# Rearranging u tile by tile, and moving the S5 steps two slots up, in a three-block fp32 kernel

## What is computed

```python
def s5_ssd_layer(h, w_in, ...):
    p = h @ w_in
    z = p[..., :o1]
    y_a = s5_mixer(p[..., o1:o2], ...)           # u: 1024 channels, 64 groups of 16
    y_a = y_a * silu(z[..., :S5_WIDTH])
    y_b = ssd_mixer(p[..., o2:o3], p[..., o3:], ...)
    y_b = rmsnorm_3(y_b * silu(z[..., S5_WIDTH:]), ssd_norm_w, SSD_GROUPS)
    return concatenate([y_a, y_b], -1) @ w_out

def s5_mixer(u, ...):
    # per group of 16 channels a complex diagonal recurrence with 64 states
    x_t = a * x_{t-1} + (coef * B) @ u_t
    y_t = real(C @ x_t)
    y = gelu(y + d_skip * u)
    return y * sigmoid(y @ glu_w + glu_b)
```

## Time and profile before

| | |
|---|---|
| median of 3 runs | 2980.46 us (2978.59 to 2983.39) |
| the profiled execution | 2977.42 us |
| its span | 2974.8 us |
| mean granted TensorE clock | 0.968 of full speed |
| TensorE matmul busy | 2803.0 us, 94% |
| VectorE, ScalarE, GpSimd busy | 48%, 34%, 38% |
| DMA | 286.21 MB, 96 GB/s; 34384 of 114251 packets under 512 B |
| `ab_in` (slots 0 to 35) | 2031.4 to 2309.3 us of the span |

### The profile page before, as it was taken

The page is one execution under the profiler, slowest core; times in us unless marked ns, Lnnn a source line. Parts: engine busy times, 40 slices in busy tenths (PEclk is TensorE's granted clock), DMA queues, the critical chain, the costliest instruction groups (busy, mean ns, idle before and its releaser), DMA issues. The chain is left out here.

```text
span 2974.8 us, 38973 instructions
## 1 busy us (share of the span) xinstructions
PE 2803.0 (94%) x16650; PEld 2300.7 (77%) x16650; DVE 1426.6 (48%) x1768; ACT 999.7 (34%) x1373; POOL 1129.7 (38%) x487
## 2 busy tenths in 40 slices
PE   7899999895899999999899999998799899999997
PEld 6778876794688888777788888886688668888785
DVE  5874338535448443873633442215287645333332
ACT  4233233113333332346432433222333644222441
POOL 3334443500244444364344444444233423322342
PEclk9999999996899999999999999999899999999998
DMA  5444222000133332222232233334855312222232
GB/s 195 148 129 148 97 94 78 31 4 1 62 113 131 110 109 90 87 91 85 71 100 92 92 99 94 98 99 144 135 163 150 105 61 89 82 65 66 69 99 71
DMA packets 114251, 286.21 MB, mean 96 GB/s; under 512 B 34384, under 2 KB 45584, under 8 KB 113424
## 3 DMA queue, kind: packets, MB, share of 16 engines
q1 hardware_dynamic: 114080, 283.74, 31.1%
HBM read 261.91 MB, written 24.15 MB: 96 GB/s over the span
## 5 line engine op out<-in xcount | busy, mean ns | idle before, releaser
L426 POOL TENSOR_TENSOR weight_ring_r<-weight_ring,weight_hi_r 128x1024 fp32r<-128x1024 f32 (+2 forms) x412 | 1043.0, 2532 | 1684.0 <-ACT weight_hi_r L419 1684.0
L419 ACT ACTIVATE weight_hi_r<-weight_ring 128x1024 fp32r<-128x1024 f32 (+2 forms) x412 | 447.7, 1088 | 1492.6 <-PE acc L629 1120.4
L623 PE MATMUL acc<-p_r,weight_hi_r 128*128 128x512 f32 x1776 | 701.4, 395 | 28.9 <-ACT weight_hi_r L419 19.4
L624 PE MATMUL acc<-scr_r,weight_hi_r 128*128 128x512 f32 x1120 | 440.5, 393 | 0.0
L629 PE MATMUL acc<-p_r,weight_ring_r 128*128 128x512 f32 x1776 | 436.6, 389 | 0.0
L623 PEld LDWEIGHTS acc<-p_r,weight_hi_r 128*128 128x128 f32 x1776 | 336.8, 190 | 103.5 <-ACT weight_hi_r L419 20.7
L624 PE MATMUL acc<-p_r,weight_hi_r 128*128 128x512 f32 x1008 | 392.1, 389 | 0.0
L629 PEld LDWEIGHTS acc<-p_r,weight_ring_r 128*128 128x128 f32 x1776 | 333.7, 188 | 69.5
L624 PEld LDWEIGHTS acc<-scr_r,weight_hi_r 128*128 128x128 f32 x1120 | 213.1, 190 | 46.1 <-issue 2.6
L623 PE MATMUL acc<-scr_r,weight_hi_r 128*128 128x512 f32 x544 | 220.2, 405 | 2.2 <-ACT weight_hi_r L419 2.2
L878 DVE SCALAR_TENSOR_TENSOR x<-acc,x 128x512 f32<-128x512 f32 x56 | 36.8, 687 | 381.9 <-PE acc L629 381.9
(11 more groups left out here) (542 smaller groups left out, 3872.7 us busy)
## 6 DMA issues: line engine op xcount, KB each, us to landing
weight_ring<-in_weights SPq DMA_DIRECT2D x372, 512.0 KB, 3.5
weight_ring<-in_weights SPq DMA_DIRECT2D x32, 704.0 KB, 4.0
weight_ring<-in_weights SPq DMA_DIRECT2D x8, 640.0 KB, 3.9
s_inner<-p SPq DMA_DIRECT2D x16, 256.0 KB, 4.3
s_outer<-p SPq DMA_DIRECT2D x16, 256.0 KB, 4.6
s_inputs<-p SPq DMA_DIRECT2D x16, 256.0 KB, 2.6
p<-s_inputs SPq DMA_DIRECT2D x8, 512.0 KB, 5.6
p<-s_inner SPq DMA_DIRECT2D x8, 512.0 KB, 4.9
```

The source lines that it names most:

```text
L419: self.nc.scalar.activation(self.r.weight_hi[:, ahead, 0:width], self.weight_ring[:, r, 0:width], ACT.Copy)\
L426: self.nc.gpsimd.tensor_tensor(rest, raw, hi, ALU.subtract).then_inc(self.weights_split, 1)
L623: pe.matmul(product.out(b, m), hi, op.hi(kx), start=kx == 0, stop=False)
L624: pe.matmul(product.out(b, m), hi, op.lo(kx), start=False, stop=False)
```

## The change

u is written to DRAM by place: for each of the eight tiles, as soon as its pair is evicted, eight DMAs (one for each place) put 128 rows of 64 numbers into `u_by_place` (SP slots 5 to 12), and in SP slots 7, 9, 11 and 13 one DMA each reads a quarter back, 4 KB from each row. The plain copy to `lift` moves to SP slots 14 to 17. V, K, the scan and Y move up: V by six to two slots, K and the scan by two, Y from twice in slots 27 and 28 to once in each of 25 to 28. `dve_skip` works in place without strides, and `act_gelu` reads with the stride and writes in token order. The dt transposes move from behind (9, 3) to behind (10, 1), the last row from (10, 1) to (10, 3). Chunk 0 of the SSD uses the odd buffers and comes first: its sums are read in SP slot 37, masked on GpSimd behind the rest of slot 35, and its exps run in the first slot of the GLU product.

```diff
@@ tables of places @@
-V_AT = ((12, 3), (13, 1), (13, 3), (14, 1))
-K_AT = ((14, 3), (15, 1), (15, 3), (16, 1), (16, 3), (17, 1), (17, 3), (18, 1))
-Y_AT = ((27, 1), (27, 3), (28, 1), (28, 3))
-SCAN_AT = {15: 2, 16: 2, 17: 2, 18: 1, 19: 2, 20: 1, 21: 2, 22: 1, 23: 2, 24: 1, 25: 1}
+V_AT = ((6, 3), (8, 3), (11, 3), (12, 1))
+K_AT = ((12, 3), (13, 1), (13, 3), (14, 1), (14, 3), (15, 1), (15, 3), (16, 1))
+Y_AT = ((25, 1), (26, 1), (27, 1), (28, 1))
+SCAN_AT = {13: 2, 14: 2, 15: 2, 16: 1, 17: 2, 18: 1, 19: 2, 20: 1, 21: 2, 22: 1, 23: 1}
@@ S5Layer.sp_slot @@
-        if at in (6, 8, 10, 12):
-            b = (at - 6) // 2
-            sp.wait_ge(core.freed["dve"], self.product.freed[b])
+        if 5 <= at < 13:
+            self.place_u(sp, at - 5)
+        if at in (7, 9, 11, 13):
+            b = (at - 7) // 2
+            sp.wait_ge(self.rows_out[b], 16 * 2 * S5_L)
+            u = core.dram["u_by_place"].rearrange("l i g n -> (l i) g n")
+            sp.dma_start(self.ul[:, 2 * S5_NB * b:2 * S5_NB * (b + 1), :], u[:, 2 * S5_NB * b:2 * S5_NB * (b + 1), :]).then_inc(self.rows_in[b], 16)
+        if 14 <= at < 18:
+            b = at - 14
             sp.dma_start(core.dram["lift"][2 * b * P:(2 * b + 2) * P, :].rearrange("(c p) t -> p c t", p=P),
                          core.p[:, S5_LIFT + 2 * b:S5_LIFT + 2 * b + 2, :]).then_inc(core.lifted, 16)
-        if at == 13:
-            sp.wait_ge(core.lifted, 16 * 4)
-            by_place = core.dram["lift"].rearrange("(g i) (l n) -> l i g n", i=S5_IN, l=S5_L)
-            for l in range(S5_L):
-                sp.dma_start(self.ul[l * S5_IN:(l + 1) * S5_IN], by_place[l]).then_inc(q["ul"], 16)
@@ S5Layer, new @@
+    def place_u(self, sp, c):
+        sp.wait_ge(self.core.freed["dve"], self.product.freed[c // 2])
+        by_place = self.core.dram["u_by_place"].rearrange("l i g n -> l g i n")
+        for l in range(S5_L):
+            sp.dma_start(by_place[l, S5_NB * c:S5_NB * (c + 1)], self.core.p[:, S5_LIFT + c, l * S5_N:(l + 1) * S5_N]).then_inc(self.rows_out[c // 2], 16)
@@ S5Layer.dve_skip, act_gelu @@
-        v.scalar_tensor_tensor(out=core.p[:, S5_GELU + c, :].rearrange("p (n l) -> p n l", l=S5_L), in0=by_run(self.u_again(c)),
-                               scalar=core.vcol("s5_d", c), in1=by_run(core.p[:, S5_UL + c, :]), op0=ALU.mult, op1=ALU.add).then_inc(self.q["skipped"], 1)
+        y = core.p[:, S5_UL + c, :]
+        v.scalar_tensor_tensor(out=y, in0=self.u_again(c), scalar=core.vcol("s5_d", c), in1=y, op0=ALU.mult, op1=ALU.add).then_inc(self.q["skipped"], 1)
-        self.core.nc.scalar.activation(y, y, ACT.Gelu_apprx_tanh).then_inc(self.q["gelu"], 1)
+        self.core.nc.scalar.activation(natural, lifted, ACT.Gelu_apprx_tanh).then_inc(self.q["gelu"], 1)
@@ SsdTimes.pe_part @@
-        if (at, part) == (9, 3):
+        if (at, part) == (10, 1):
             pe.wait_ge(q["sums"], 1)
+            pe.wait_ge(self.v_read, 4)
...
-        if (at, part) == (10, 1):
+        if (at, part) == (10, 3):
...
         if (at, part) == V_AT[0]:
+            pe.wait_ge(q["step"], 1)
+        if (at, part) == V_AT[2]:
             pe.wait_ge(q["exps"], 1)
@@ Ssd.sp_sums, GpSimd and ScalarE in block3_second @@
-            sp.wait_ge(layer.q["skipped"], DC)
+            sp.wait_ge(layer.q["gelu"], 2)
-    sums_at = {38: 1, 39: 0, 44: 2, 46: 3}
+    sums_at = {37: 0, 39: 1, 44: 2, 46: 3}
-                    if product is glu and at in (0, 1, 6):
-                        ssd.pool_mask(pool, {0: 1, 1: 0, 6: 2}[at])
+                    if (product, at) == (ab.product, 34):
+                        ssd.pool_mask(pool, 0)
+                    if product is glu and at in (1, 6):
+                        ssd.pool_mask(pool, {1: 1, 6: 2}[at])
+                if at == 0:
+                    ssd.act_exps(act, 0)
                 if at == 2:
-                    ssd.act_exps(act, 0)
+                    ssd.act_exps(act, 1)
                     ssd.act_copy(act, 0)
-                if at == 4:
-                    ssd.act_exps(act, 1)
```

More of the change, by code:

```diff
@@ L2706, in __init__ @@
         p, h, cst = core.p, core.h, core.cst
-        names = ("tables", "ul", "v", "v_read", "k", "k_read", "step", "y", "added", "u_back", "skipped", "gelu")
+        names = ("tables", "v", "v_read", "k", "k_read", "step", "y", "added", "u_back", "skipped", "gelu")
         self.q = {n: core.sem(f"sl_{n}") for n in names}
-        self.loaded, self.inner, self.outer = ([core.sem(f"sl_{n}{j}") for j in range(S5_PIECES)] for n in ("inputs", "inner", "outer"))
-        self.kept, self.back = ([core.sem(f"sl_{n}{j}") for j in range(S5_PIECES // 2)] for n in ("kept", "back"))
+        self.piece_in = [core.sem(f"sl_piece{j}") for j in range(S5_PIECES)]
+        self.rows_out, self.rows_in = ([core.sem(f"sl_rows_{n}{j}") for j in range(S5_PIECES // 2)] for n in ("out", "in"))
         flat = lambda a: a.rearrange("p a t -> p (a t)")
@@ L2740, in sp_slot @@
[L2740 to L2748 removed]
+        if at in (12, 13, 15, 16):
+            first = (0, 2, 4, 6)[(12, 13, 15, 16).index(at)]
+            for j in (first, first + 1):
+                sp.wait_ge(q["v"], j + 1)
+                sp.dma_start(self.place[j], piece("inner", j)).then_inc(self.piece_in[j], 16)
@@ L3459, in dve_slot @@
         layer = self.layer
-        if at in (27, 28, 29):
-            layer.dve_add(dve, (0, 2, 3)[at - 27])
+        if 25 <= at < 29:
+            layer.dve_add(dve, at - 25)
         if at == 35:
@@ L3589, in _ @@
             for s in core.flow_loads(sp, flow):
-                if s < ab.product.end:
+                if s < ab.product.end + RING:
                     ab.sp_slot(sp, s - flow.first)
```

80 lines of the change are left out of this document (35 added, 45 removed).

## The result

The changed kernel takes 2965.4 us in the median of 7 runs (2963.8 to 2966.8), the kernel before 2980.3 in its 7 (2971.7 to 2983.4). The ratio is 0.9959, with a 95% interval of 0.9949 to 0.9969: 9 to 15 us faster. The forecast was 2953. The sign is right and the time lies in the range, but by the ratio the kernel gained about half of what the sum promised (12 us of 26).

The account below looks back on a forecast made before the run. TensorE, busy 94% of the span, was taken as the bound, so only its waits pay: -15.4 in front, -10.8 at the back and 0 in SSD take 2977.4 to 2951.2 us, given as 2953, range 2943 to 2968.

Parts of the forecast that it names:

- Front: TensorE's stalls around V and the dt transposes: 19.3 us before, 3.9 after, a gain of 15.4 (bounds 9 and 19).
- the exps at the third V pair: ScalarE runs the dt exps only after rounding slot 12's weights, so TensorE waits 1.9 us at the third V pair.
- The last row read: SP's last read of u, queued behind the writes, lands 0 to 5.5 us late for TensorE; 2 taken.
- so I take 0.56: On SP, one 256 B-row write of u costs 0.56 us, like `keep`'s writes, so SP keeps up with TensorE.
- that rule: DMA writes below 512 B do a read-modify-write; the last row read would come 10.6 us later, the sum about 2962.
- Give nothing for the clock behind a stall that short: At GLU's start, no time was counted for slow matmuls behind a stall of 0 to 6 us.
- I take 3: TensorE's stall at GLU's start is 0 to 6 us, taken as 3, for a back-half gain of 10.8.
- Rival 1: Masks and a weight subtraction on GpSimd slow VectorE's last taps; GLU stall 6 us or more, time 2957, chance 0.2.
- signs that I had named for being wrong: TensorE waiting for weights in slots 5 to 13, writes over 1 us on SP, or 9 us taps with GLU stall over 6.
- V, K and the scan keep their distances to each other, so the 2.0 us ahead of Y stay: TensorE's 2.0 us wait ahead of the first Y matmuls remains, and so does the slow clock behind it.
- SSD at 0: Moving the first mask and exps ahead of the GLU gates changes nothing in the SSD part, bounds +2 and -1.3.
- The sum: Whole kernel: -15.4 in front, -10.8 at the back, 0 in SSD, together -26.2 us from 2977.4 to 2951.2.

Follow-up runs that it names:

- e2: The kernel before with the DRAM tensor for u in its new order allocated but unused; ratio to the kernel before 0.9996.
- e8: The changed kernel with each of the 64 writes of u cut into two halves of 64 partitions; ratio to the kernel before 0.9995.
- e3: The changed kernel with GpSimd's first masks back in slot 0 of the GLU product; 2960.0 us, ratio to the kernel before 0.9928.
- e13: The changed kernel with its back half as before (Y, output, skip, GELU) and the first masks in GLU slot 0; ratio to the kernel before 0.9924.
- e15: The changed kernel with Y half a slot later (part 3 instead of 1 of slots 25 to 28); 2951.4 us, ratio to the kernel before 0.9905.
- e11: The changed kernel with the first masks in GLU slot 0 and the dt exps one slot earlier; ratio to the kernel before 0.9926.
- e17: The changed kernel with its back half as before, masks in GLU slot 0 and the dt exps one slot earlier; ratio to the kernel before 0.9921.
- e16: The changed kernel with Y half a slot later, masks in GLU slot 0 and dt exps one slot earlier; ratio to the kernel before 0.9905.
- e4: The changed kernel with the strides back on VectorE (skip and GELU as in the kernel before); 2963.3 us, ratio to the kernel before 0.9941.

## Why the prediction was right in front and wrong at the back

- **Front: right.** I gave 19.3 us before and 3.9 after. A to B fell from 274.5 to 259.9 (means of two and three traces), 14.7, against 15.4. The 19.3 came from one trace; in e2's the wait ahead of V is 13.4 instead of 15.7. The stall left over is the one that I named, the exps at the third V pair: 1.9 to 2.5 us of wait and 1.5 of slow clock. The last row read, for which I took 2, was in time. The step "so I take 0.56", the price of a write, was the one that carried this half (0.61 measured), and e8 shows what hung on it. No row shows a read-modify-write for the 256 B writes: SP issued the last row read, which waits for them, 2.9 us behind the last of them (2121.82 and 2124.68), so the sum with that rule, 2962, was not needed.
- **"Give nothing for the clock behind a stall that short"**, at the back. Wrong: the matmuls behind 5.35 us took 3.3 too many in one trace and 1.7 in the two others, those behind the 2.5 us wait 1.5. At the third V pair I had left out the same term, and the read that came in time covered it; that was luck.
- **"I take 3" for the stall at GLU's start.** Wrong: 5.35 + 1.00 of wait. This is the step that failed: with the slow matmuls behind it the stall cost 8.0 to 9.6 us instead of 3, 5 to 6.6 too many, and the stage missed its forecast by 5.6. Rival 1 named the mechanism and the size: it prices the stall at 13.8 - 5 = 8.8 us, and its gain of 20.4 stands beside the 20.6 of A to C. The taps began where I had put them, 4.7 us ahead of ab_in's end (forecast 5.0 to 6.5); it is their length that I had wrong. I had written down that taps beside GpSimd took 4.7 us too much, saw that the change puts both the masks and a weight subtraction beside them, and still took a stall from the middle, for taps of between 4.5 and 9.2 us. The nearest row was the one of the same instructions beside GpSimd, 9.22; it came out as 9.19. I had also misread what ran beside that row: two weight subtractions and two and a half masks. Read rightly, it would have said what e3 shows, that the weight subtractions make most of the excess (3.7 of 4.9 us) and that moving the masks alone would not have saved the forecast. The 1.00 behind it had no term at all: the fourth subtraction for GLU's inputs took 2.86 us instead of 0.69 beside a weight subtraction. Of the signs that I had named for being wrong, the last came true: taps of 9 us, and a stall of over 6.
- **"V, K and the scan keep their distances to each other, so the 2.0 us ahead of Y stay."** Right in its own terms (2.4 and a slow clock), but I took it for a wait with a price of 2 and no part of the change. It costs 6 us with the clock, and it is the change that keeps it: e13 has none of it, and e15 removes it with half a slot. The back half gained 7.5 us at GLU's wait against e13 (11.7 to 4.2, with e3's masks) and paid 5.1 ahead of B (258.8 against 253.7). So with Y where the change has it the back half is worth 1.4 us in A to C (e3 against e13) or 3.8 (e11 against e17), and nothing that the ratios can tell (0.9928 for e3, 0.9924 for e13, each to some 0.0014). With Y half a slot later it is worth 8.2 (e16 against e17).
- **SSD at 0.** The wait there fell from 5.0 to 3.6, about as bounded (-1.3). What I had no term for is the clock behind it: C to end rose by 5.0 us in the mean of the traces. Whether the change causes that, or three traces happened on the bad side, stays open: single traces of one kernel differ by 6 us there. Of the 17 traces with u by place, six lie from 588.5 to 591.0, about where the two of before are, four from 592.7 to 593.3, and seven from 595.3 to 598.7.
- **The sum.** -26.2 forecast; -20.6 in the stage, -15.6 with the part behind C, -9 to -15 and -13 to -22 by the intervals of the changed kernel's first and second series of runs. By parts: 14.7 in front (forecast 15.4), 4.2 to 5.8 at GLU's start (10.8), 1.4 at the wait of the SSD part (0). Rival 1, with its 20.4, was the stage's gain, and the clock behind C is what neither it nor my case had.

The best version is e15, one number per place of Y changed: about 28 us under the kernel before (ratio 0.9905; e16 has the same) and 11 to 16 under the changed one by the ratios (0.9905 against 0.9942, 0.9949 and 0.9959).

## What to carry to other kernels

Price an operation by the row in which it already ran beside the same neighbour, not by its row alone, and give the slow matmuls behind a wait a term of their own (0 to 3.7 us here). When a chain is moved up as a whole, look again at the waits that its inner distances cause: half a slot ahead of Y was worth as much here as the rest of the back half (4.4 and 3.8 us in A to C). Test the halves of a change apart, and compare traces between fixed points of the program, since a spread of 10 us outside the changed stage hides a gain of 5.

## What the runs showed that was not expected

- The same program, up to the same matmul, took from 2029.4 to 2039.8 us. The instructions between 680 and 800 us, mostly small matmuls with short waits, found granted clocks from 0.63 to 0.71 there.
- Behind one and the same 3.6 us wait (L3176), the clock stayed at its lower level for some 5 us in one trace and some 16 in another of the same kernel.
- What SP pays for a DMA does not follow its bytes: 0.61 us for a write of 128 rows of 256 B, 0.56 for one of 64 rows, and 0.46 for a read of 128 rows of 4 KB, sixteen times the bytes. A read of 1024 rows of 256 B took 2.35.
- VectorE and GpSimd can stretch each other to about double: six taps take 4.29 us alone, 6.43 beside one weight subtraction, 8.01 beside two, 9.19 beside two and four masks. One weight subtraction, 2.4 us otherwise, took 5.47 in e4, beside the strided skip and the taps of 2287.42:

```profile
2285.61 5.47 POOL L427 TENSOR_TENSOR weight_ring_r<-weight_ring,weight_hi_r 128x1024 fp32r<-128x1024 f32 x1 [3.03 <-ACT weight_hi_r L420]
```
